# A ten-stage transformer kernel: another split of mixer 2's output product, 512-column down products, rounded masks and another placing of the modulation

## The chip, the cores and the metric

One core of one Trainium2 chip. Time is device microseconds of one execution. The kernel before ran three times: 1709.82, 1713.06 and 1714.77 us, median 1713.06.

## The reference

Two blocks of two layers each work on x (256 tokens by 1024), all in float32:

```
for l in 0, 1:                       # first block
    x += 0.5 * gate * swiglu(norm_mod(x))        # "ffn"
    x += gate * mixer(norm_mod(x))               # "mix1": recurrence, stick-breaking and forgetting attention
    x += 0.5 * gate * swiglu(norm_mod(x))        # "ffn"
for l in 0, 1:                       # second block
    x += gt1 * (group_rmsnorm([pool, chunk attention, top-k attention, latent attention]) @ w_out)   # "mix2"
    x += gt2 * ((silu(h @ w1) * (h @ w3)) @ w2)  # "ffn"
return rmsnorm(x)
```

Shifts, scales and gates of every norm come from `silu(c) @ w_ada` and `silu(c_2) @ w_mod`: 120 panels of 1 MB ("modulation").

## The kernel before, in words

The ten stages run in the order of SUBS: ffn, mix1, ffn, ffn, mix1, ffn, mix2, ffn, mix2, ffn (numbers 0 to 9). The work of each engine is written out by hand in one order, and the engines meet by semaphores.

x stands turned (features on partitions) as eight chunks X[:, c, :] of 128x256. Every large product is made exact with rounded operands: a weight w becomes WH (rounded to fp32r, by ScalarE, `hi_half`, L1146) and WL = w - WH (by VectorE, `lo_half`, recorded at L1602), an activation likewise HH and HL, AH and AL or YH and YL. One 128x128 block of weights then takes three matmuls of 256 columns: WH by AH, WH by AL, WL by AH. Weights come in units of 1 MB (two halves of eight blocks each) through `ring`, four slots filled by the sync queue in the order of `loads`; WH and WL hold four halves. A slot is free once VectorE has taken the remainders of its unit, or has used a modulation panel.

An ffn has 33 units: 22 for the up products (`cols`), 11 for the down product (`out_proj`, L661): eight output chunks c, each a sum over 22 blocks k, in PSUM banks 4, 5, 0, 1, 2, 3. `residual` on VectorE (L1689) adds each finished chunk to X, once, with the gate. Then `gained` makes the rounded operand of the next stage. Six stages are ffns, so there are six down stages of 176 blocks.

The modulation panels are multiplied and summed by VectorE (`ada_half`, L1629), 1024 columns at a time, at fixed ticks of the stages: ADA_N says how many panels a stage has, `ada_halves` at which tick. Eight more come at the start.

A mixer has 14 units: ten projections, four of the output product. `out_round` (L611) makes the output product in two rounds. A round sums over some of the eight input chunks for all eight output chunks. VectorE adds a chunk's first sum to X in `partial` and its second in the last loop, each followed by `gained`. In mix2, round 0 takes chunks 6, 7, 0, 1, 4, 5 and round 1 chunks 2, 3. The attention tiles behind a chunk must be normalised, turned and rounded before it can be used: `tile_scale` (ScalarE), `diagonal` (VectorE), `turned_out` (TensorE), `tile_out` (ScalarE), `tile_rest` (VectorE). Six attention scores with their softmax go through banks 2 and 3 one after the other (`mla_score`, `sa_score`, `ca_score`, then `maxima2`, `exponents2`, `turn`, `by_keys`, `attend`, `attended2`). All that order stands in mixer2 of TensorE (L1080 to L1098), ScalarE (L1514 to L1534) and VectorE (L2074 to L2116).

Masks are added to the scores as a matmul of the identity by the mask in full fp32 (`fox_score`, `stick_sums`, `sa_score`). Such a matmul stands in the trace as two instructions.

Of the kernel before, what the change touches and what calls it, by code (L numbers as in the profile page):

```python
# [14 lines left out]
S = 256  # L15
# [3 lines left out]
BIG = 1.0e30  # L19
# [10 lines left out]
def columns(spec):  # L30
    at, out = 0, {}
    for name, n in spec:
# [5 lines left out]
CONST_SPEC = [("ident", 128), ("ones", 128), ("eps", 1), ("one", 1), ("bd", 128), ("ntri", 128), ("partner", 96), ("rev", 128), ("cos", 256), ("sin", 256),  # L38
              ("cnt", 512), ("causal", 128), ("nones", 128), ("chunk", 256), ("sbpos", 128), ("sb01", 128),
              ("onehot", 320)]  # L40
CONST, NCONST = columns(CONST_SPEC)
FIRST = CONST["bd"]
# [15 lines left out]
ADA_N = (21, 3, 20, 20, 3, 20, 3, 20, 2, 0)  # L58
# [10 lines left out]
ROUNDS = {"mix1": ((0, 1, 2, 3), (6, 7, 4, 5)), "mix2": ((6, 7, 0, 1, 4, 5), (2, 3))}  # L69
# [5 lines left out]
def ada_halves(n, t):  # L75

    first = FIRST_ADA + sum(ADA_N[:n])
    halves = range(2 * ADA_N[n])
    if SUBS[n][0] == "ffn":
        at = [q for q in halves if 3 + q * (NTICK["ffn"] - 3) // len(halves) == t]  # L80
    else:
        at = [q for q in halves if ADA_AT[SUBS[n][0]][q // 2] == t]
    return [(first + q // 2, q % 2) for q in at]


def build(nc, A):
    ctx = ExitStack()
    with ctx:
# [15 lines left out]
        SQ = sb("SQ", [128, KD, S])  # L104
        CN = sb("CN", [128, NCONST])
        VC = sb("VC", [128, NVEC])
# [8 lines left out]
        AH = nc.alloc_sbuf_tensor_at("AH", [128, NF, S], F32R, offset=scr_at)  # L115
        AL = nc.alloc_sbuf_tensor_at("AL", [128, NF, S], F32R, offset=scr_at + 4 * NF * S)
# [25 lines left out]
        s_lam, s_lame, s_wfa = sem("s_lam"), sem("s_lame"), sem("s_wfa")  # L142
# [32 lines left out]
        eps = const("eps")  # L175
        one = const("one")
# [99 lines left out]
        SC = [scr(128), scr(256)]  # L276
        WK = [scr(128), scr(256)]
        CQ = v3(scr(512), 2)
# [65 lines left out]
        def summed2(n, r, c):  # L344
# [5 lines left out]
            if SUBS[n][0] == "mix1":  # L350
                return s_op2, 8 * SUBS[n][1] + 4 * r + c // 2 + 1
            return s_op2, 16 + 12 * SUBS[n][1] + 6 * r + c + 1 - (c > 3)
# [25 lines left out]
        def _(e):  # L378
            e.dma_start(VC[:, :], A["vecs"]).then_inc(s_vec, 16)
            e.dma_start(CN[:, 0:FIRST], A["consts"][:, 0:FIRST]).then_inc(s_const, 16)  # L380
# [7 lines left out]
            for p, (kind, i) in enumerate(loads):  # L388
# [16 lines left out]
                if p == 14:  # L405
                    e.dma_start(CN[:, FIRST:], A["consts"][:, FIRST:]).then_inc(s_const_rest, 16)
# [98 lines left out]
        def _(e):  # L505
# [139 lines left out]
            def turned_back(c):  # L645

                e.wait_ge(*((s_xg, c + 1) if c < KD - 1 else (s_xgl, 1)))
                for t in range(2):
                    last = e.transpose(PS[:, (6 if c < 4 else 0) + t, 128 * (c % 4):128 * (c % 4) + 128], XG[:, c, 128 * t:128 * t + 128], ident)
# [11 lines left out]
            def out_proj(n, xh, xl, ready):  # L661
# [4 lines left out]
                for i in range(KD * kt):  # L666
# [32 lines left out]
            def ffn(n):  # L699
# [10 lines left out]
                out_proj(n, lambda k: AH[:, k, :], lambda k: AL[:, k, :], lambda k: e.wait_ge(s_al, NF * j + k + 1))  # L710

            def mixer1(n):
# [32 lines left out]
                def fox_score(t):  # L745
# [3 lines left out]
                    for h in range(0, 4, per):  # L749
                        mm(s3[:, h:h + per, 128 * t:128 * t + 128], ident,  # L750
                           causal.rearrange("p (o k) -> p o k", o=1).to_broadcast([128, per, 128]), start=True, stop=False, skip=True)
# [5 lines left out]
                def fox_turn(t):  # L757

                    e.wait_ge(s_aex, a0 + t + 1)
                    for kt in range(t + 1):  # L760
# [6 lines left out]
                        for h in range(4):  # L767
                            last = e.transpose(PS[:, 6 + r % 2, 128 * h:128 * h + 128], softmax_of(t)[:, h, 128 * kt:128 * kt + 128], ident)
# [21 lines left out]
                def stick_sums(p):  # L790
                    e.wait_ge(s_zs, 2 * l + p + 1)
                    for h in (2 * p, 2 * p + 1):
# [3 lines left out]
                        last = mm(v3(c, 3)[:, 0:3:2, :], ident,  # L796
                                  const("sbpos").rearrange("p (o k) -> p o k", o=1).to_broadcast([128, 2, 128]),
# [68 lines left out]
            def mixer2(n):  # L866
# [32 lines left out]
                def index_rows():  # L899

                    for t in range(2):
                        last = e.transpose(PS[:, 7, 128 * t:128 * t + 128], SKI[:, 128 * t:128 * t + 128], ident)
# [1429 lines left out]
```

## Time and profile before

| | |
|---|---|
| median of three runs | 1713.06 us |
| profiled execution, its own time | 1709.39 us |
| its span | 1707.6 us |
| TensorE matmul busy | 1635.3 us, 96% |
| VectorE busy | 1313.3 us, 77% |
| ScalarE busy | 913.9 us, 54% |
| mean granted clock of TensorE | 0.984 |
| DMA | 403.22 MB, mean 236 GB/s |

The stages stand in the span in this order. The starts are those of the first product of each, read from the timeline: ffn 0 at 38, mix1 at 226, ffn 2 at 345, ffn 3 at 534, mix1 at 723, ffn 5 at 842, mix2 at 1032, ffn 7 at 1174, mix2 at 1365, ffn 9 at 1506 us. The down products are the last 62 us of each ffn. Busy time of TensorE counts overlapping matmuls once, so the number of instructions in a stretch tells more than the share.

### The profile page before, as it was taken

How to read it: one execution, taken by the hardware profiler on the slowest of the kernel's cores; microseconds unless marked ns; L12 is line 12 of the kernel's file. 1: busy time of each engine (PE TensorE's matmuls, PEld its weight loads, DVE VectorE, ACT ScalarE, POOL GpSimd, SP SyncE). 2: the span in 40 equal slices, each digit the busy share in tenths (PEclk: the TensorE clock that was granted, in tenths of full speed). 3: DMA queues.
4: the chain of work that ended last, by engine and by line, in shares of the span. 5: the costliest groups of instructions: out<-in, count | busy, mean ns of one | idle time of the engine just before them, and what ended most of it. 6: DMA issues, size and time to landing. Idle time of an engine off the chain costs nothing.

```text
span 1707.6 us, 31946 instructions
## 1 busy us (share of the span) xinstructions
PE 1635.3 (96%) x13290; PEld 1604.8 (94%) x13290; DVE 1313.3 (77%) x2071; ACT 913.9 (54%) x1564; POOL 84.0 (5%) x124
## 2 busy tenths in 40 slices
PE   2999999999999999999999999979999999899998
PEld 2999998999999999998999999978999998899998
DVE  6688898788788878897788888847888898385553
ACT  5445458664445544477554545646545456464453
POOL 4000000000000000000110001001000010010000
PEclk8999999999999999999999999989999999999999
DMA  9787765348786778754378888313778773145451
GB/s 357 301 317 300 300 253 198 124 178 336 294 317 261 300 300 316 290 210 173 115 271 312 305 318 301 124 50 117 301 300 319 296 250 124 50 149 197 176 196 50
DMA packets 57168, 403.22 MB, mean 236 GB/s; under 512 B 6606, under 2 KB 6866, under 8 KB 9280
## 3 DMA queue, kind: packets, MB, share of 16 engines
q1 hardware_dynamic: 55424, 396.01, 61.6%
q0 software_dynamic: 1600, 5.18, 1.0%
q8 instruction: 105, 1.72, 0.4%
q14 instruction: 39, 0.32, 0.1%
HBM read 400.10 MB, written 1.05 MB: 235 GB/s over the span
## 4 chain that ended last, share of the span: by engine, by line
PE 81%; DVE 11%; ACT 4%; issue 2%; DMA 1%; SPq 0%; DVEq 0%; ACTq 0%
PE PS L507 81%; DVE WL L1602 3%; DVE SCR L1602 2%; DVE SCR L1605 1%; ACT WH L1146 1%; DVE ring L1629 1%; ACT SCR L1429 1%; DMA SCR<-in_x 1%; DVE X L1605 1%; DVE HL L1605 1%; DVE SCR L1599 1%; DVE SMALL L1984 1%; DMA ring<-in_win 0%; ACT HH L1178 0%; DVE SCR L1946 0%
## 5 line engine op out<-in xcount | busy, mean ns | idle before, releaser
L1602 DVE TENSOR_TENSOR WL<-ring,WH 128x1024 fp32r<-128x1024 f32 (+1 forms) x508 | 599.8, 1215 | 187.4 <-ACT WH L1146 186.8
L507 PE MATMUL PS<-HH,WH 128*128 128x256 f32 (+1 forms) x2640 | 651.5, 285 | 12.7 <-ACT WH L1146 9.5
L507 PE MATMUL PS<-HL,WH 128*128 128x256 f32 (+1 forms) x2640 | 640.1, 283 | 0.0
L1146 ACT ACTIVATE WH<-ring 128x1024 fp32r<-128x1024 f32 (+1 forms) x508 | 510.9, 1048 | 100.1 <-PE PS L507 39.7
L507 PEld LDWEIGHTS PS<-HH,WH 128*128 128x128 f32 x2640 | 497.2, 190 | 18.8 <-ACT WH L1146 9.7
L507 PEld LDWEIGHTS PS<-HL,WH 128*128 128x128 f32 x2640 | 495.1, 190 | 0.7
L507 PE MATMUL PS<-HH,WL 128*128 128x256 f32 (+1 forms) x2640 | 375.9, 280 | 2.3 <-DVE WL L1602 2.2
L507 PEld LDWEIGHTS PS<-HH,WL 128*128 128x128 f32 x2640 | 339.4, 189 | 3.7 <-DVE WL L1602 3.7
L1629 DVE CUSTOM_DVE_ANT_0 ring<-ring,CB,VC 128x1024 f32<-128x1024 f32 x240 | 316.4, 1339 | 9.0 <-DMA ring<-in_ada 8.9
L507 PE MATMUL PS<-AH,WH 128*128 128x256 f32 x1056 | 297.5, 282 | 0.0
L507 PE MATMUL PS<-AL,WH 128*128 128x256 f32 x1056 | 297.0, 281 | 0.0
L507 PE MATMUL PS<-AH,WL 128*128 128x256 f32 x1056 | 297.0, 281 | 0.0
L507 PEld LDWEIGHTS PS<-AL,WH 128*128 128x128 f32 x1056 | 203.1, 192 | 0.0
L507 PEld LDWEIGHTS PS<-AH,WL 128*128 128x128 f32 x1056 | 199.0, 188 | 0.0
L507 PEld LDWEIGHTS PS<-AH,WH 128*128 128x128 f32 x1056 | 199.0, 188 | 0.0
L1204 ACT ACTIVATE AH<-SCR 128x256 fp32r<-128x256 f32 x132 | 55.2, 418 | 224.8 <-DVE SCR L1602 214.5
L1230 ACT ACTIVATE SCR<-PS 128x256 f32<-128x256 f32 x122 | 46.5, 381 | 114.5 <-PE PS L507 60.9
L437 POOL TENSOR_TENSOR SQ<-SQ 128x256 f32<-128x256 f32 x54 | 41.9, 776 | 1294.7 <-ACT SQ L1162 1292.5
L507 PE MATMUL PS<-SCR 128*128 128x64 f32 (+4 forms) x528 | 89.0, 315 | 5.9 <-DVE SQ L1602 4.4
L507 PEld LDWEIGHTS PS<-SCR 128*128 128x128 f32 (+1 forms) x528 | 77.1, 197 | 14.5 <-issue 8.7
L1605 DVE SCALAR_TENSOR_TENSOR X<-PS,MOD,X 128x256 f32<-128x256 f32 x112 | 53.0, 478 | 47.8 <-PE PS L507 47.5
L1159 ACT ACTIVATE HH<-X,AB 128x256 fp32r<-128x256 f32 x72 | 36.5, 506 | 93.2 <-DVE X L1605 92.7
(206 smaller groups left out, 1488.0 us busy)
## 6 DMA issues: line engine op xcount, KB each, us to landing
ring<-in_up SPq DMA_DIRECT2D x88, 1024.0 KB, 5.6
ring<-in_ada SPq DMA_DIRECT2D x72, 1024.0 KB, 7.2
ring<-in_ffn SPq DMA_DIRECT2D x66, 1024.0 KB, 4.8
ring<-in_mod SPq DMA_DIRECT2D x48, 1024.0 KB, 6.9
ring<-in_down SPq DMA_DIRECT2D x44, 1024.0 KB, 6.5
ring<-in_win SPq DMA_DIRECT2D x32, 1024.0 KB, 6.9
ring<-in_wout SPq DMA_DIRECT2D x16, 1024.0 KB, 4.8
ring<-in_winv SPq DMA_DIRECT2D x4, 1024.0 KB, 4.8
```

What stands on the lines that cost most here:

```text
L437: e.tensor_tensor(SQ[:, c, :], SQ[:, c - 1, :], SQ[:, c, :], ALU.add).then_inc(s_psum, 1)
L507: return e.matmul(out, lhsT, rhs, start=start, stop=stop, skip_group_check=skip)
L1146: e.activation(half_of(i)[0], slot_of(("unit", u))[:, w * (i % 2):w * (i % 2) + w], ACT.Copy).then_inc(s_hi, 1)
L1159: e.activation(HH[:, c, 0:S], X[:, c, :], ACT.Copy, scale=AB[:, 8 * m + c:8 * m + c + 1]).then_inc(s_yh, 1)
L1204: e.activation(AH[:, f, :], G6[:, 3 + f % 3, :], ACT.Copy).then_inc(s_ah, 1)
L1230: e.activation(G6[:, f % 3, :], PS[:, up_bank(f), 0:256], ACT.Silu).then_inc(s_silu, 1)
L1429: last = e.activation(p3[:, h, :], s3[:, h, :], ACT.Exp, bias=st[:, at + h:at + h + 1], scale=scale, accum_out=st[:, 8 + h:9 + h])
L1599: return e.tensor_scalar(out, a, s1, s2, op0) if s2 is None else e.tensor_scalar(out, a, s1, s2, op0, op1)
L1602: return e.tensor_tensor(out, a, b, op)
L1605: return e.scalar_tensor_tensor(out=out, in0=a, scalar=s, in1=b, op0=op0, op1=op1)
L1629: ins = e.tensor_tensor_reduce(out=w, in0=w, in1=CB[:, 0 if i < 72 else 1, :], scale=1.0, scalar=bias, op0=ALU.mult, op1=ALU.add, accum_ou ...
L1984: ins = e.tensor_reduce(st[:, 0:4], score_bank(n, 2, t), AX.X, ALU.max, negate=True)
```

## The change

- The down products of output chunks 0 to 6 take AH and AL side by side (new layout AHL) as one 512-column matmul by WH, then WL by AH on the first 256 columns. The two halves of the bank are added to X by two instructions instead of one. Chunk 7 is left as it was.
- mix2: round 0 takes chunks 6, 7, 0, 1 and round 1 chunks 4, 5, 2, 3. The last two scores, three `attend`, two `turn` and four `turned_out` are issued between the output chunks of round 0. On ScalarE and VectorE roundings of output weights (units u0+10 to u0+14) are moved around them, in part by halves.
- identity, causal mask, stick-breaking mask and the top-k mask are rounded to fp32r (BIG becomes a power of two), so that mask products are fp32r. Transposes read the same identity bits as fp32.
- ADA_N: from (21, 3, 20, 20, 3, 20, 3, 20, 2, 0) to (22, 2, 20, 21, 0, 22, 0, 21, 0, 4). The four of the last ffn lie in its up products.

```diff
-ADA_N = (21, 3, 20, 20, 3, 20, 3, 20, 2, 0)
+ADA_N = (22, 2, 20, 21, 0, 22, 0, 21, 0, 4)
-ROUNDS = {"mix1": ((0, 1, 2, 3), (6, 7, 4, 5)), "mix2": ((6, 7, 0, 1, 4, 5), (2, 3))}
+ROUNDS = {"mix1": ((0, 1, 2, 3), (6, 7, 4, 5)), "mix2": ((6, 7, 0, 1), (4, 5, 2, 3))}
 # out_proj, TensorE
-                    mm(out, wh[:, g, :], xh(k), start=k == 0, stop=False)
-                    mm(out, wh[:, g, :], xl(k), start=False, stop=False)
+                    if c < KD - 1:
+                        both = PS[:, banks[c % len(banks)], :]
+                        mm(both, wh[:, g, :], AHL[:, k, :, :].rearrange("p a s -> p (a s)"), start=k == 0, stop=k == kt - 1, skip=True)
+                    else:
+                        mm(out, wh[:, g, :], AH[:, k, :], start=k == 0, stop=False)
+                        mm(out, wh[:, g, :], AL[:, k, :], start=False, stop=False)
...
-                    last = mm(out, wl[:, g, :], xh(k), start=False, stop=k == kt - 1)
+                    last = mm(out, wl[:, g, :], AH[:, k, :], start=False, stop=k == kt - 1, skip=c < KD - 1)
 # residual, VectorE
-                stt(X[:, c, :], PS[:, banks[c % 6], 0:256], MOD[:, 24 * n + 16 + c:24 * n + 17 + c], X[:, c, :], ALU.mult,
+                b = (4, 5, 0, 1, 2, 3)[c % 6]
+                if c < KD - 1:
+                    step(stt(X[:, c, :], PS[:, b, 256:512], MOD[:, 24 * n + 16 + c:24 * n + 17 + c], X[:, c, :], ALU.mult, ALU.add))
+                stt(X[:, c, :], PS[:, b, 0:256], MOD[:, 24 * n + 16 + c:24 * n + 17 + c], X[:, c, :], ALU.mult,
                     ALU.add).then_inc(s_x, 1)
 # sa_score; fox_score and stick_sums likewise
-                        mm(s3[:, h:h + per, :], ident, WK[t][:, 0:m].rearrange("p (o k) -> p o k", o=1).to_broadcast([128, per, m]),
+                        mm(s3[:, h:h + per, :], identr[:, :], WKR[t][:, :].rearrange("p (o k) -> p o k", o=1).to_broadcast([128, per, m]),
 # mixer2, TensorE
-                turned_out(n, o0 + 4)
-                e.wait_ge(s_toe_ca, 64 * (l + 1))
-                e.wait_ge(s_proj, p0 + 10)
-                ca_score(a0 + 4, 0)
-                attend(a0 + 3, 1, r0 + 6, o0 + 5, of_sa)
-                turn(a0 + 4, 0, r0 + 6)
-                ca_score(a0 + 5, 1)
-                attend(a0 + 4, 0, r0 + 7, o0 + 6, of_ca)
-                turned_out(n, o0 + 5)
+                e.wait_ge(s_proj, p0 + 9)
                 out_round(n, 0, {
-                    1: (lambda: turned_out(n, o0 + 6),),
-                    2: (lambda: turn(a0 + 5, 1, r0 + 7),),
-                    4: (lambda: attend(a0 + 5, 1, r0 + 9, o0 + 7, of_ca),),
+                    0: (lambda: e.wait_ge(s_toe_ca, 64 * (l + 1)), lambda: e.wait_ge(s_proj, p0 + 10), lambda: ca_score(a0 + 4, 0)),
+                    1: (lambda: attend(a0 + 3, 1, r0 + 6, o0 + 5, of_sa), lambda: turn(a0 + 4, 0, r0 + 6), lambda: ca_score(a0 + 5, 1)),
+                    2: (lambda: attend(a0 + 4, 0, r0 + 7, o0 + 6, of_ca), lambda: turned_out(n, o0 + 4), lambda: turn(a0 + 5, 1, r0 + 7)),
+                    3: (lambda: attend(a0 + 5, 1, r0 + 9, o0 + 7, of_ca),),
+                    4: (lambda: turned_out(n, o0 + 5),),
+                    5: (lambda: turned_out(n, o0 + 6),),
                     6: (lambda: turned_out(n, o0 + 7),),
                 })
 # mixer2, ScalarE: hi(u0 + 11) no longer ahead of tile_out(o0 + 3)
-                hi(u0 + 11)
                 tile_out(n, o0 + 3)
                 by_keys(r0 + 4, 0, a0 + 3)
                 by_keys(r0 + 5, 1, a0 + 3)
-                tile_out(n, o0 + 4)
+                hi_half(2 * u0 + 22)
                 exponents2(a0 + 4, 0, 1.0, r0 + 4)
+                hi_half(2 * u0 + 23)
...
 # mixer2, VectorE
                 selected(1)
+                lo(u0 + 10)
                 pooled(1, o0 + 3)
-                lo(u0 + 10)
                 tile_rest(n, o0 + 1)
...
+                maxima2(a0 + 3, 1)
                 diagonal(n, o0 + 4)
-                maxima2(a0 + 3, 1)
+                gates(n)
                 tile_rest(n, o0 + 3)
-                lo(u0 + 11)
-                tile_rest(n, o0 + 4)
+                lo_half(2 * u0 + 22)
                 maxima2(a0 + 4, 0)
+                partial(n, 0)
+                lo_half(2 * u0 + 23)
```

Not shown: the order of the constants in their tensor, three short roundings of constants on ScalarE in ffn 0, and the placing of the last units' roundings, which for u0+14 becomes that of mix1.

## Rows read from the trace of the kernel before

**Rows 1.** The page: busy time, share and instructions of TensorE; the chain's engines.
```profile
PE 1635.3 (96%) x13290; PEld 1604.8 (94%) x13290; DVE 1313.3 (77%) x2071; ACT 913.9 (54%) x1564; POOL 84.0 (5%) x124
...
PE 81%; DVE 11%; ACT 4%; issue 2%; DMA 1%; SPq 0%; DVEq 0%; ACTq 0%
```
**Rows 2.** Windows: length, busy PE PEld DVE ACT POOL (count), clock, DMA.
```profile
163.80:226.00 62.20, 62.20 (x530) 62.20 (x530) 52.46 (x72) 29.89 (x40) 4.43 (x6) 1.00 0.78 308
...
1032.16:1174.50 142.34, 130.57 (x974) 123.48 (x973) 101.21 (x218) 77.54 (x191) 6.55 (x10) 0.95 0.43 148
1364.62:1505.94 141.32, 130.41 (x975) 123.56 (x973) 98.70 (x214) 77.64 (x191) 6.54 (x10) 0.95 0.40 142
...
722.67:842.40 119.73, 113.71 (x872) 108.14 (x870) 94.91 (x156) 81.09 (x149) 4.47 (x5) 0.99 0.45 163
1126.70:1174.50 47.80, 40.89 (x314) 39.28 (x313) 23.48 (x48) 24.58 (x67) 1.48 (x2) 0.93 0.25 86
...
1131.00:1137.00 6.00, 5.22 (x25) 5.25 (x25) 3.97 (x7) 1.59 (x4) 0.00 (x0) 0.50 0.34 108
```
**Rows 3.** Waits of TensorE in mix2, 1104 to 1174.5: total us, times, longest.
```profile
PE PS L507 <- DVE YL L1605: 6.8, 3, 3.4
...
PE PS L507 <- DVE X L1605: 1.8, 2, 1.3
```
**Rows 4.** The chain of waits in mix2: start, us, what.
```profile
1112.40 0.33 DVE SQ L1602
1112.73 1.69 DVE WL L1602 x2
...
1129.31 1.04 ACT WH L1146
...
1131.78 7.02 PE PS L507 x36
```
**Rows 5.** Timeline of TensorE: start, time, matmul, tiles, shape, count.
```profile
1148.12 0.28 PE L507 MATMUL PS<-YH,WH 128*128 128x256 f32 x1
...
1148.69 0.28 PE L507 MATMUL PS<-YH,WL 128*128 128x256 f32 x1
...
1430.44 1.02 PE L507 MATMUL PS<-SCR,CN 128*128 128x512 f32 x2
1431.31 0.38 PE L507 MATMUL PS<-SCR 128*128 128x128 f32 x2
...
259.82 0.28 PE L507 MATMUL PS<-HH,WFH 128*4 128x256 f32 x1
...
260.75 0.28 PE L507 MATMUL PS<-HH,WFH 128*4 128x256 f32 x1
```
**Rows 6.** The page's groups: loads of 128 weight columns, mean ns.
```profile
L507 PEld LDWEIGHTS PS<-AH,WL 128*128 128x128 f32 x1056 | 199.0, 188 | 0.0
```
**Rows 7.** The tile WFH: loads of 4 weight columns, ns min/median/max.
```profile
L507 PEld LDWEIGHTS PS<-HH,WFH x16: 83/84/85, 259.7 to 757.9; 128*4 128x4 f32 x16
```
**Rows 8.** Groups of VectorE in the first down stage, 163.8 to 226.
```profile
L1602 DVE TENSOR_TENSOR WL<-ring,WH 128x1024 fp32r<-128x1024 f32 x22 | 26.0, 1216 | 2.0 <-ACT WH L1146 1.9
L1629 DVE CUSTOM_DVE_ANT_0 ring<-ring,CB,VC 128x1024 f32<-128x1024 f32 x15 | 21.8, 1474 | 0.0
...
L1605 DVE SCALAR_TENSOR_TENSOR X<-PS,MOD,X 128x256 f32<-128x256 f32 x7 | 3.3, 478 | 2.6 <-PE PS L507 2.6
```
**Rows 9.** Waits of all engines in the same stretch.
```profile
ACT WH L1146 <- DMA ring<-in_down: 12.6, 7, 4.5
DVE HL L1605 <- ACT HH L1159: 3.5, 6, 0.6
```
**Rows 10.** The chain of waits in the second mix1.
```profile
760.97 1.20 DVE ring L1629
...
762.17 1.20 DVE ring L1629
```
**Rows 11.** Timeline of ScalarE in the second mix1.
```profile
763.71 1.72 ACT L1336 ACTIVATE SCR<-SCR,SMALL 128x256 f32<-128x256 f32 x4
```

More of the change, by code:

```diff
@@ L79, in ada_halves @@
     if SUBS[n][0] == "ffn":
-        at = [q for q in halves if 3 + q * (NTICK["ffn"] - 3) // len(halves) == t]
+        ticks = NF - 3 if n == NSUB - 1 else NTICK["ffn"] - 3
+        at = [q for q in halves if 3 + q * ticks // len(halves) == t]
     else:
@@ L104, in build @@
         SQ = sb("SQ", [128, KD, S])
+        cn_at = nc.sbuf_base
         CN = sb("CN", [128, NCONST])
+        identr, causalr, sbposr = (nc.alloc_sbuf_tensor_at(k + "r", [128, 128], F32R, offset=cn_at + 4 * CONST[k])
+                                   for k in ("ident", "causal", "sbpos"))
         VC = sb("VC", [128, NVEC])
@@ L276, in build @@
         SC = [scr(128), scr(256)]
+        wk_at = scr_at + 4 * Scratch.at
         WK = [scr(128), scr(256)]
+        WKR = [nc.alloc_sbuf_tensor_at(f"WKR{t}", [128, 128 * (t + 1)], F32R, offset=wk_at + 512 * t) for t in range(2)]
         CQ = v3(scr(512), 2)
@@ L648, in turned_back @@
                 for t in range(2):
-                    last = e.transpose(PS[:, (6 if c < 4 else 0) + t, 128 * (c % 4):128 * (c % 4) + 128], XG[:, c, 128 * t:128 * t + 128], ident)
+                    last = e.transpose(PS[:, (6 if c < 4 else 0) + t, 128 * (c % 4):128 * (c % 4) + 128], XG[:, c, 128 * t:128 * t + 128], ident1)
                 if c % 4 == 3:
@@ L659, in token_sums, with out_proj @@
                     last.then_inc(s_fss, 1)
[L661 removed]
+            def out_proj(n, ready):
                 kt = depth_of(n)
@@ L749, in fox_score @@
                     for h in range(0, 4, per):
-                        mm(s3[:, h:h + per, 128 * t:128 * t + 128], ident,
-                           causal.rearrange("p (o k) -> p o k", o=1).to_broadcast([128, per, 128]), start=True, stop=False, skip=True)
+                        mm(s3[:, h:h + per, 128 * t:128 * t + 128], identr[:, :],
+                           causalr[:, :].rearrange("p (o k) -> p o k", o=1).to_broadcast([128, per, 128]), start=True, stop=False, skip=True)
                     for h in range(4):
@@ L1226, in ffn @@
                         e.activation(CB[:, 1, :], CB[:, 1, :], ACT.Silu).then_inc(s_cb, 1)
+                        e.wait_ge(s_const_rest, 16)
+                        for exact, k in ((identr, "ident"), (causalr, "causal"), (sbposr, "sbpos")):
+                            e.activation(exact[:, :], const(k), ACT.Copy).then_inc(s_exact, 1)
                     if f >= 3:
@@ L2090, in mixer2 @@
                 attended2(a0 + 4, o0 + 6)
-                tile_rest(n, o0 + 5)
+                partial(n, 2)
+                tile_rest(n, o0 + 4)
                 diagonal(n, o0 + 6)
-                gates(n)
-                partial(n, 0)
-                lo(u0 + 12)
-                partial(n, 1)
-                tile_rest(n, o0 + 6)
-                partial(n, 2)
                 partial(n, 3)
                 attended2(a0 + 5, o0 + 7)
+                lo_half(2 * u0 + 24)
                 partial(n, 4)
+                tile_rest(n, o0 + 5)
                 diagonal(n, o0 + 7)
                 partial(n, 5)
-                lo(u0 + 13)
+                tile_rest(n, o0 + 6)
+                lo_half(2 * u0 + 25)
                 partial(n, 6)
```

59 lines of the change are left out of this document (32 added, 27 removed).

## The prediction

> **What bounds the kernel now.** I read the page first: TensorE is busy for 96% of the span and the chain that ended last lies for 81% on it [rows 1]. So time goes only where TensorE does less, or where it waits. Second, the windows by stage [rows 2]. In a down stage the clock is 1.00 and TensorE has no pause: 530 matmuls in 62.20 us, 117.4 ns from start to start. An ffn can gain only by fewer or shorter products. The mixers are different: mix2 takes 142.34 and 141.32 us at a mean clock of 0.95, and VectorE is busy for 101.21 of the 142. Third, the waits of TensorE and the chain inside mix2 [rows 3, 4] say where those pauses are.
>
> The sum goes by the profiled execution: 1709.39 us, 1.8 us more than its span. The median of the runs is 1713.06, 3.7 above it, and I put the saving under the median.
>
> **Wide down products.** Chunks 0 to 6 of 22 blocks in six stages are 7 x 22 x 6 = 924 blocks. Before, a block costs three matmuls, 3 x 117.4 = 352 ns [rows 2]. After, it costs one of 512 columns and one of 256. No fp32r matmul of 512 columns stands in the trace, so I bound it. 256 columns at 2.4 GHz are 107 ns, so 10 ns of the 117 are something else. The mask products of 512 columns in fp32 start 1431.31 - 1430.44 = 0.87 us apart for two instructions, 0.435 us each [rows 5], at two clocks per column (427 ns): there only some 8 ns come on top of a stream twice as long as that of a 512-column fp32r product. Is the weight load the limit? A load of 128 columns takes 188 ns and one of 4 columns 84 [rows 6, 7], 104 ns less, but the products with the 4-column weights still follow each other at (260.75 - 259.82) / 8 = 116 ns [rows 5]. So the load is hidden and a longer stream hides it as well. In the output rounds the pitch is (1148.69 - 1148.12) / 5 = 114 ns [rows 5]. If the extra 10 ns belongs to the columns, the wide product costs 235 and nothing is gained. If nothing came on top of the stream, the block would cost 320 and save 32 ns. The nearest rows say half an fp32 instruction, 218 ns, and 115 for the narrow one: 333, a saving of 19 ns. 924 x 19 = 17.6 us. Ends: 0 and 29.6 us.
>
> The Trainium skill, "TensorE: Matmul & The Clock Gate", section "Back-to-back issue gap", gives N/2.4 + 2.5 ns once warm, so 109 and 216 ns. The trace does not agree at 256 columns (117.4). By that rule a block would cost 325 ns, the saving would be 25 us and the total some 7 us lower than mine; it is a rival below.
>
> What hides the second addition to X? VectorE. It is busy for 52.46 of the 62.20 us [rows 2]. Seven more additions of 478 ns [rows 8], less where they overlap, with seven waits for the first one to finish, are 3.2 us. The moved modulation adds up to one panel of two instructions per down stage, 2 x 1.47 = 2.9 us at the mean [rows 8]. VectorE then has 56 to 59 us of work and still waits 3.5 us in all for ScalarE's HH [rows 9], while TensorE would need only 62.2 - 154 x 0.019 = 59.3 us. That is too tight for nothing to show. What is queued behind the new wait on VectorE is the next `lo_half`, `gained` and the modulation, and by the modulation the slots of the ring. ScalarE already waits 12.6 us for panels in the first down stage [rows 9]. The four halves of WH and WL cover delays of a few us. I charge 0.6 us for each of the five down stages that have modulation, 3 us in all (ends 0 and 10). Net of the wide products: 14.6 us.
>
> **Masks in fp32r.** One fp32 mask product of 512 columns costs 0.87 us [rows 5], in fp32r 0.22 (from the 218 above); one of 256 costs half, 0.43, against 0.115. In mix1 the causal masks are 1 x 512 and 2 x 256, the stick-breaking ones 4 x 256: 0.65 + 6 x 0.32 = 2.5 us per mixer, 5.0 for both. There TensorE runs without pause, but one later wait is for VectorE, so I keep 4 us (ends 2 and 5). In mix2 there are three of 512 columns: 2 us per mixer, counted below. Transposes cost what they did.
>
> **Modulation out of the mixers.** In the second mix1 two modulation instructions of 1.20 us stand in the chain of waits [rows 10], inside a stretch in which only VectorE moves. Without them the chain is 2.4 us shorter, until ScalarE's exponentials (763.71 + 1.72 = 765.43 [rows 11]) end last; VectorE used them at 767.62, so the gain is 2.2 us. The first mix1 keeps its two panels on that place and gains nothing. In mix2 the three panels stand early, where TensorE is mostly busy: 0.3 us each. The panels themselves cost nothing in up products, where VectorE has room, and the four in the last ffn end before its gates are needed. Sum 2.8 us.
>
> **mix2's tail.** The window from 1126.70 to the end is 47.80 us with 314 matmuls [rows 2]. Of these 192 belong to the output rounds, 192 x 0.1155 = 22.2 us. The other 122 are fp32 instructions of the late attention, 114 at about 0.11 and 8 of 256 columns at 0.216: 14.3 us. Work is 36.5 us, so 11.3 us are waits and half clock. Two of the three waits for YL, 5.1 of the 6.8 us, and 1.8 us for X [rows 3] lie there, and the clock is 0.50 from 1131 to 1137 [rows 2], which costs 3 us. Small restarts, 1.4 us, make up the rest.
>
> What follows in the new order, step by step:
> - Before, `turned_out(o0+4)` waited until 1131.78, since `tile_rest(o0+3)` stood behind two ScalarE roundings of unit u0+11, the second at 1129.31 [rows 4]. They now come after `tile_out(o0+3)`, so YL is ready 2.1 us earlier, and TensorE has chunks 6 and 7 of the first output to do meanwhile. About 0.8 of 3.5 us is left.
> - `ca_score(a0+4)` then runs. While VectorE and ScalarE make its softmax (0.7 + 1.5 us), TensorE does output chunk 1 and `attend(a0+3)`, 3.2 us of work: hidden.
> - `ca_score(a0+5)` takes 3.5 us; its softmax (1.2 + 1.9 us) lies beside chunk 2 (1.4), `attend(a0+4)` (0.9) and `turned_out(o0+4)` (0.4): 0.5 us late for `turn(a0+5)`.
> - ScalarE must then do `tile_scale`, `tile_out` and two `by_keys`, 2.8 us, beside `turn` and chunk 3 (2.3): 0.5 us late. Every later `turned_out` has a chunk of 1.4 us ahead of it.
> - Round 1 has four products per chunk, 1.4 us, against the 0.9 us that VectorE needs for X and HL. Before it had 0.7 us, which is where the waits for X came from. The next ffn starts 0.5 us quicker.
> - TensorE no longer stands for 3 us, so I expect the second half-clock stretch to go.
>
> New tail: 36.5 + 0.8 + 0.5 + 0.5 + 1.2 of restarts = 39.5 us, 8.3 less, and 0.5 in the next ffn. Ahead of the tail, the masks save 2 us, but `lo(u0+10)` now stands before `pooled(1)`. In the chain it was 1112.40 for `pooled`, then the rounding [rows 4]. The new order delays `pooled(1)` by 2.3 us, and behind it ScalarE's `tile_scale(o0+3)` and `tile_out(o0+1)`, so `turned_out(o0+2)` comes 1.7 us later. Net 0.3. Per mix2 9.1 us, for both 18.2 (ends 9 and 25).
>
> **Sum.** 14.6 + 4 + 2.8 + 18.2 = 39.6 us. 1709.4 - 39.6 = 1669.8 beside the profile, 1713.1 - 39.6 = 1673.5 as a median.
>
> **Rivals.**
> - The extra 10 ns belongs to the columns. For it: it is in every fp32r stream, with full and with 4-column weights. Against it: fp32 streams have only 8 ns on 427. The wide products then give nothing, and the additional work on VectorE 1 us: 1713.1 - 25.0 + 1.0 = 1689. Chance 0.14.
> - Nearly nothing comes on top of a stream once the weight load has time: 325 ns a block, 25 us, which VectorE then limits to about 20: 1668, and with the full mixer gain 1662. Chance 0.20. This is also what the skill's rule would give.
> - The late attention only moves its waits: in round 0 `turn(a0+5)` and `attend(a0+5)` wait for a ScalarE that is now behind with halves of weights, and the half clock stays. Mix2 then gives 3 us each: 1713.1 - 39.6 + 12.2 = 1686. For it: softmax takes 3.1 us per step and only 2.7 lie beside it. Chance 0.12.
> - Slower: VectorE becomes the bound of the down stages. Its 56 to 59 us plus 3.5 of waits reach 62.5, more than the 62.2 of now; TensorE then waits in pieces, and if such a wait brings a stretch at 1.2 GHz like that from 1131 to 1137 [rows 2], 3 us more are lost. The mixers and masks give 25 us, so it decides from 4.2 us lost in each of six stages. At 5 us each (2 of waits and 3 of clock): 1713.1 - 25 + 30 = 1718. Against it: the clock is 1.00 in the whole stage, and four halves lie ready. Chance 0.03.
>
> My own forecast has 0.51. A difference of over 0.3%, 5 us, can be told from no change. Faster by more than that: 0.95; within it 0.02; slower 0.03. The range takes in the first three rivals and half of the bounds: 1654 to 1692.
>
> **What would show it.** In the changed profile: 512-column matmuls from AHL with starts about 218 ns ahead of the next; down stages of 59 to 60 us with the clock at 1.00; VectorE busy for over 90% of them; mix2 of about 132 us, with waits for YL of under 2 us and no half clock in its last 40 us; mask products of 0.22 us; no modulation in the second mix1 which takes 115 to 116 us instead of 119.7. I am wrong if the wide product starts 235 ns ahead of the next, if TensorE waits over 2 us for WL in the down stages, or if mix2 stays above 137 us.

## The result and the profile after

The changed kernel takes 1691.84 us (median of 4 runs, 1688.75 to 1694.38), the kernel before in the same comparison 1713.91 (1709.82 to 1714.86). The ratio is 0.9876, 95% interval 0.9864 to 0.9887: 22 us faster, where 39.6 was forecast. The profiled execution took 1691.13 us, against 1709.39 of the one before: 18.3 us less. What follows explains these 18.3; the medians are 3.8 further apart. The profiled execution of the kernel before, 1709.39 us, was faster than all four of its timed runs.

The page of the changed kernel answers to [rows 1]: 944 fewer matmuls and weight loads (924 by the wide products, 20 by the masks), and only 13.7 us less busy time of TensorE. The second line is the group of products from the new layout AHL: 924 of 512 columns and 264 of 256.

```profile
PE 1621.6 (96%) x12346; PEld 1552.1 (92%) x12346; DVE 1333.8 (79%) x2113; ACT 912.1 (54%) x1567; POOL 85.0 (5%) x124
...
L516 PE MATMUL PS<-AHL,WH 128*128 128x512 f32 (+1 forms) x1188 | 373.5, 371 | 0.0
```

Windows of the changed kernel, with the columns of [rows 2]: the first down stage, that of ffn 5, the second mix1, the first mix2, its tail, the second mix2.

```profile
163.81:228.63 64.82, 62.99 (x377) 55.09 (x375) 55.70 (x78) 28.68 (x40) 4.43 (x6) 1.00 0.81 306
967.87:1032.08 64.21, 62.59 (x377) 54.93 (x375) 55.46 (x78) 28.89 (x40) 4.44 (x6) 1.00 0.80 311
723.91:838.98 115.07, 110.44 (x865) 105.18 (x863) 90.02 (x147) 81.92 (x150) 4.21 (x5) 1.00 0.41 150
1032.08:1164.93 132.85, 125.77 (x972) 121.16 (x970) 96.79 (x208) 78.75 (x193) 8.69 (x12) 0.97 0.37 130
...
1125.67:1164.93 39.26, 37.99 (x315) 36.72 (x313) 24.53 (x47) 24.98 (x68) 3.63 (x4) 1.00 0.23 81
...
1354.76:1487.92 133.16, 126.06 (x972) 121.42 (x971) 96.15 (x208) 79.08 (x193) 8.90 (x12) 0.96 0.37 129
```

The down stage has lost 153 matmuls and got 2.6 us longer than the 62.20 of [rows 2]. The first mix2 is 9.5 us shorter. Its tail, from `turned_out(o0+3)` on in both kernels (1126.7 before, 1125.67 now), is 39.26 us at full clock instead of 47.80 at 0.93.

With every stage taken from the start of its first product to that of the next one's, and without the 18.1 us before TensorE's first instruction (18.2 now), the account is this:

| us | before | after | measured | forecast |
|---|---|---|---|---|
| six down stages (the last with the final norm) | 384.6 | 389.4 | +4.8 | -14.6 |
| four mixers (with masks and modulation) | 521.9 | 497.7 | -24.2 | -25.0 |
| six up stages | 782.9 | 784.0 | +1.1 | 0 |
| span | 1707.6 | 1689.3 | -18.3 | -39.6 |

No product of the up stages is changed. Their lengths differ by 1.5 us between profiles, also where they are the same code (that of ffn 3 takes 126.2 or 127.7 us), because 256-column products follow each other for long stretches sometimes at 113, sometimes at 118 ns.

Timeline of TensorE in the first down stage of the changed kernel (start, time, matmul, tiles, shape, count):

```profile
169.80 0.40 PE L516 MATMUL PS<-AHL,WH 128*128 128x512 f32 x1
170.04 0.28 PE L516 MATMUL PS<-AHL,WL 128*128 128x256 f32 x1
170.16 0.40 PE L516 MATMUL PS<-AHL,WH 128*128 128x512 f32 x1
170.39 0.28 PE L516 MATMUL PS<-AHL,WL 128*128 128x256 f32 x1
```

Only the starts are to be read. Over the stretches looked at (325 blocks) the wide product starts 235 ns ahead of the next, the narrow one 118. A block costs 353 ns, as before. That is rival 1.

The narrow products have a second pace, which the wide ones don't reach. In chunk 7 of the last down stage of the changed kernel, with full clock, three of them take 1675.17 - 1674.83 = 0.34 us, 113 ns each:

```profile
1674.83 0.39 PE L516 MATMUL PS<-AHL,WH 128*128 128x256 f32 x2
1675.06 0.28 PE L516 MATMUL PS<-AHL,WL 128*128 128x256 f32 x1
1675.17 0.39 PE L516 MATMUL PS<-AHL,WH 128*128 128x256 f32 x2
```

In the kernel before 80 of the 176 blocks of that stage take 340 ns, in e10, with three products of the same size from AHL, none. The blocks with a wide product stay at 353 in all stages but for single ones. So beside the faster pace the wide form costs 13 ns a block. What chooses the pace is not shown.

Waits of the first down stage (engine, tile, line, waited for: us in total, times, longest):

```profile
ACT WH L1155 <- DMA ring<-in_down: 15.1, 6, 5.1
...
DVE WL L1617 <- ACT WH L1155: 2.9, 2, 1.5
PEld PS L516 <- DVE WL L1617: 2.7, 3, 1.6
PE PS L516 <- DVE WL L1617: 1.8, 2, 1.3
```

The chain of the end of the same stage (start, us, what) shows how that comes about:

```profile
206.90 1.69 DVE ring L1644
...
208.63 4.92 DMA ring<-in_down
...
213.58 1.07 ACT WH L1155
...
214.67 2.36 DVE WL L1617 x2
217.03 0.41 DVE X L1620
...
217.47 0.49 DVE X L1620
```

A slot of the ring comes free only when VectorE has used the panel in it (206.90). The next unit lands 4.92 us later, ScalarE rounds it, VectorE takes the remainder, and only then come the two additions to X. Each further instruction on VectorE delays the slot, and the DMA turns that into a later WL. TensorE then stands before a product that needs WL. In the whole kernel it waited for WL 4 times before, 2.2 us in all, and now 10 times, 6.9 us.

Waits of TensorE in the first mix2 from 1104 us on; they answer to [rows 3]:

```profile
PE PS L516 <- DVE SQ L1617: 4.7, 1, 4.7
PE PS L516 <- DVE YL L1620: 0.9, 2, 0.6
PE PS L1008 <- ACT SCR L1441: 0.6, 1, 0.6
```

The 6.8 us for YL and 1.8 for X have gone down to 0.9. The wait for SQ, 2.2 us before, has become 4.7: `attend(a0+2)` waits for `pooled(1)`, as e4 and e10 bear out.

### The profile page after: what moved, and what is told of

Its sections match the earlier page's. It is cut to its first block, busy times and chain, and to the rows that moved or that the text cites. A ratio compares the mean times of both kernels' runs of the same rounds, so it can differ in the third digit from the quotient of the medians.

```text
span 1689.3 us, 30111 instructions
## 1 busy us (share of the span) xinstructions
PE 1621.6 (96%) x12346; PEld 1552.1 (92%) x12346; DVE 1333.8 (79%) x2113; ACT 912.1 (54%) x1567; POOL 85.0 (5%) x124
## 4 chain that ended last, share of the span: by engine, by line
PE 77%; DVE 13%; ACT 5%; DMA 3%; issue 1%; SPq 0%; DVEq 0%; ACTq 0%
PE PS L516 76%; DVE WL L1617 4%; DVE ring L1644 2%; ACT WH L1155 2%; DMA ring<-in_down 1%; DVE X L1620 1%; DVE SCR L1617 1%; DVE SCR L1620 1%; DVE HL L1620 1%; DMA SCR<-in_x 1%; ACT SCR L1441 1%; DVE SCR L1614 1%; DVE SMALL L2001 1%; DMA ring<-in_win 0%; ACT HH L1168 0%
## 5 line engine op out<-in xcount | busy, mean ns | idle before, releaser
L516 PE MATMUL PS<-AHL,WH 128*128 128x512 f32 (+1 forms) x1188 | 373.5, 371 | 0.0
L516 PE MATMUL PS<-AHL,WL 128*128 128x256 f32 x1056 | 297.4, 282 | 4.0 <-DVE WL L1617 3.9
L516 PEld LDWEIGHTS PS<-AHL,WH 128*128 128x128 f32 x1188 | 213.8, 188 | 42.2
L516 PEld LDWEIGHTS PS<-AHL,WL 128*128 128x128 f32 x1056 | 198.3, 188 | 6.4 <-DVE WL L1617 6.1
L1213 ACT ACTIVATE AHL<-SCR 128x256 fp32r<-128x256 f32 x132 | 55.1, 418 | 225.3 <-DVE SCR L1617 215.1
L1620 DVE SCALAR_TENSOR_TENSOR X<-PS,MOD,X 128x256 f32<-128x256 f32 x154 | 73.3, 479 | 25.4 <-PE PS L516 22.9
L516 PE MATMUL PS<-YH,WH 128*128 128x256 f32 x256 | 73.8, 288 | 1.1 <-DVE YL L1620 1.1
L516 PE MATMUL PS<-YL,WH 128*128 128x256 f32 x256 | 71.5, 279 | 0.0
```

Source lines behind the costliest of these rows:

```text
L516: return e.matmul(out, lhsT, rhs, start=start, stop=stop, skip_group_check=skip)
L1213: e.activation(AH[:, f, :], G6[:, 3 + f % 3, :], ACT.Copy).then_inc(s_ah, 1)
L1620: return e.scalar_tensor_tensor(out=out, in0=a, scalar=s, in1=b, op0=op0, op1=op1)
```

## The experiments

All compare with the kernel before, run beside them on the same chip. "Changed" is the changed kernel, and each diff is against it, except where it says before. This table gives the stage lengths from each profile, in us; the text refers to it.

| kernel | ratio, 95% | down 0 | down 5 | mix1 | mix1 | mix2 | mix2 |
|---|---|---|---|---|---|---|---|
| before | 1 | 62.2 | 62.2 | 118.5 | 119.7 | 142.3 | 141.3 |
| changed | 0.9876 (0.9864-0.9887) | 64.8 | 64.2 | 116.6 | 115.1 | 132.9 | 133.2 |
| e1 narrow | 0.9843 (0.9829-0.9858) | 62.3 | 62.4 | 116.6 | 115.8 | 132.1 | 133.7 |
| e2 old modulation | 0.9865 (0.9847-0.9883) | 62.7 | 62.2 | 116.6 | 118.3 | 132.5 | 133.6 |
| e3 one addition | 0.9838 (0.9823-0.9853) | 62.2 | 62.2 | 116.6 | 115.8 | 132.5 | 132.3 |
| e4 pooled first | 0.9857 (0.9835-0.988) | 64.6 | 64.2 | 118.3 | 115.9 | 130.6 | 130.8 |
| e5 wide alone | 1.0004 (0.9991-1.0017) | 62.6 | 62.2 | 118.6 | 118.6 | 142.4 | 141.5 |
| e6 mix2 alone | 0.9907 (0.9893-0.992) | 62.2 | 62.2 | 119.6 | 118.6 | 134.6 | 134.0 |
| e7 masks alone | 0.9964 (0.9949-0.998) | 62.2 | 62.2 | 116.6 | 116.7 | 140.6 | 138.8 |
| e9 narrow, pooled first | 0.9826 (0.9813-0.984) | 62.2 | 62.2 | 117.8 | 115.8 | 131.3 | 130.3 |
| e10 early pooled | 0.9813 (0.98-0.9827) | 62.2 | 62.2 | 118.2 | 115.8 | 129.1 | 127.9 |
| e11 no modulation in mix1 | 0.9822 (0.9808-0.9835) | 62.2 | 62.2 | 120.0 | 114.7 | 128.5 | 128.0 |

### Which factor lengthens the down stages: e1, e2, e3

e1, the down products narrow and one addition per chunk:
```diff
-                    if c < KD - 1:          # out_proj: wide product
+                    if c < 0:
...
-                if c < KD - 1:              # residual: two additions
+                if c < 0:
```


> The changed kernel with three 256-column down products and one addition per chunk again; all else as changed. The theory (fp32r costs by the column, the second addition makes VectorE late): down stages 0 and 5 fall from 64.8 and 64.2 us to below 63, no product waits for WL in them, and the total is 4 to 6 us below the changed kernel, ratio to before 0.984 to 0.985. Rival (the 22 panels of modulation alone make VectorE late): those stages stay above 64 us and the total stays at 0.987 to 0.988. Rival (the wide product does save time): total above 1692 us.

Measured: 1688.38 us, ratio 0.9843. Its timeline in the first down stage, with the layout AHL and two narrow products where the wide one was:

```profile
170.02 0.28 PE L516 MATMUL PS<-AHL,WL 128*128 128x256 f32 x1
170.13 0.40 PE L516 MATMUL PS<-AHL,WH 128*128 128x256 f32 x2
170.37 0.28 PE L516 MATMUL PS<-AHL,WL 128*128 128x256 f32 x1
170.49 0.40 PE L516 MATMUL PS<-AHL,WH 128*128 128x256 f32 x2
```

Two products of 256 columns take the 235 ns of the wide one. TensorE doesn't wait for WL in that stage any more, though it has 22 panels: panels alone don't make VectorE late. The wide form gains nothing, and taking it out with its second additions gives back 3.5 us by the medians and 5.7 by the ratios.

e2, the modulation as before:
```diff
-ADA_N = (22, 2, 20, 21, 0, 22, 0, 21, 0, 4)
+ADA_N = (21, 3, 20, 20, 3, 20, 3, 20, 2, 0)
```


> The changed kernel with the modulation panels at their old places (21, 3, 20, 20, 3, 20, 3, 20, 2, 0). The theory (22 panels and two additions together are too much): down stages 0 and 5 at 62.3 to 62.8 us, but the second mix1 2 us longer again, mix2 up to 1 us: total within 2 us of the changed kernel. Rival (the second addition alone does it): the down stages 0 and 5 stay above 64 us and the total is 2 to 3 us above the changed kernel.

Measured: 1691.13 us, as the changed kernel. The down stages 0 and 5 fall to 62.7 and 62.2, and the second mix1 rises to 118.3 (in part by two stretches of 3.4 us at half clock, which the changed kernel's profile doesn't have): the one pays for the other.

e3, the wide products kept, but only the first half of each bank is added to X, so that the part from AL is left out of the result for these chunks:
```diff
-                if c < KD - 1:              # residual: two additions
+                if c < 0:
```


> The changed kernel, but only the first 256 columns of a wide sum are added to X: the part WH by AL is left out of X. The theory (VectorE's second addition is the cost): down stages as in e1, 62.2 to 62.6 us, total as e1 within 1.5 us. Rival (a 512-column product holds TensorE or a bank longer than two of 256): down stages 0 and 5 above 64 us.

Measured: 1686.98 us, 0.9838. The window of its first down stage:

```profile
163.80:226.00 62.20, 62.20 (x377) 55.07 (x376) 53.13 (x73) 29.45 (x40) 4.43 (x6) 1.00 0.82 319
```

377 matmuls without a pause in the same 62.20 us as the 530 of [rows 2]. That is the cleanest reading of the case: with no wait at all the wide products save nothing. The rival, that a wide product holds TensorE or a bank longer, is out for this pace. The lengthening needs both the second additions and 22 panels in the stage; without either it is at most 0.5 us.

### Each part alone: e5, e6, e7

e5 is the kernel before with the wide products and their two additions only; e6 is before with the new rounds and orders of mix2 only; e7 is before with the rounded masks only.

> The kernel before with the 512-column down products and their second addition alone; modulation, masks and mix2 as before. The theory (fp32r costs by the column, 235 and 118 ns a block as before; the additions only fill VectorE): down stages 62.2 to 63 us, total 0 to 3 us above the kernel before. Rival (my prediction's step, 19 ns a block saved, hidden in the changed kernel by late weights): down stages near 60 us and the total 10 us or more lower.

> The kernel before with the two rounds of four chunks and the late attention steps of mix2 alone. By the prediction: each mix2 7 us shorter (8.8 without the 2 us of masks), total 14 to 16 us less, ratio 0.991. Rival (the order helps only with the masks and without modulation in the mixer): each mix2 less than 5 us shorter.

> The kernel before with the fp32r masks alone. By the prediction: each mix1 2.0 to 2.5 us and each mix2 about 2 us shorter, 8 us in all, ratio 0.995. Rival (VectorE and ScalarE pace the mixers there): less than 4 us in all.

Measured: 1713.34, 1696.19 and 1707.05 us. The wide products are worth 0 (interval -0.9 to +1.7 thousandths, that is -1.5 to +2.9 us). The new order of mix2 shortens the two stages by 7.7 and 7.3 us, the masks the four mixers by 1.9, 3.0, 1.7 and 2.5 us. These four add up to 9.1 us, the ratio says 6.2 (3.4 to 8.7): the profiled execution of e7 was its fastest. Not all of the 3.0 belongs to the masks, since the kernel before has a stretch of 3.4 us at half clock in its second mix1, and e7 has none. Without any, and without the new masks, that stage takes 118.6 us in e5 and in e6, and the first mix1 of e5 too:

```profile
227.33:345.95 118.62, 112.68 (x873) 107.07 (x872) 97.07 (x158) 82.02 (x150) 4.28 (x5) 1.00 0.47 170
```
```profile
721.33:838.05 116.72, 110.34 (x865) 105.48 (x863) 95.57 (x157) 80.96 (x149) 4.22 (x5) 1.00 0.46 167
```

The first line is the first mix1 of e5, the second the second mix1 of e7, both at clock 1.00. At equal clock the masks are worth 1.9 to 2.0 us in each mix1. In mix2, e7's second stretch at half clock is 3.4 us long instead of 6.8, which is part of its 1.7 and 2.5.

The three ratios multiply to 0.9875, and the changed kernel has 0.9876. That leaves nothing for the new placing of the modulation, but the intervals together allow 4 to 5 us either way. The direct comparison is e2, where the down stages take what the second mix1 gets.

### The wait before attend(a0+2): e4, e9, e10

e4 (and e9, with narrow products besides):
```diff
                 selected(1)
-                lo(u0 + 10)
                 pooled(1, o0 + 3)
+                lo(u0 + 10)
```


> The changed kernel with VectorE's rounding of unit u0+10 behind the first pooled(1) again, as before the change. The theory (in the changed trace TensorE stands for 4.9 us before attend(a0+2), which waits for that pooled(1)): this wait falls to 2.5 us, the next one grows from 0.6 to about 1.3, and each mix2 is 1.5 us shorter: total 3 us less, ratio 0.985 to 0.986. Rival (VectorE has the same work either way and TensorE waits for the later tile_rest): total unchanged within 1 us.

Measured: 1691.3 us. Its waits in the same part of the first mix2:

```profile
PE PS L516 <- DVE SQ L1617: 2.5, 1, 2.5
PE PS L516 <- DVE YL L1620: 1.8, 3, 1.0
```

The wait for `pooled(1)` is 2.5 us again, and 0.9 us of the gain comes back as waits for YL. The mix2 stages are 2.3 and 2.4 us shorter, more than the 1.3 that the two waits give. In the second, the half-clock stretch is 6.8 us long instead of 10.2. The median doesn't show it (1685.9 to 1694.2 is a wide scatter, and this profile has two stretches of 3.4 us at half clock in the first mix1 where the changed kernel's has none), and the ratios 0.9857 and 0.9876 have intervals that overlap; the stages and e9 do show it.

> The changed kernel with narrow down products and, in the second mixer, pooled(1) before lo(u0+10) instead of behind it. Theory (the two costs are separate: the wide products' waits in down stages 0 and 5, and the remainder of FeedForward chunk 10 that delays pooled(1)): down stages 0 and 5 at 62.2 to 62.4 us, second mixers 130.6 to 131 us each, that is 3.5 us for the first and 2 x 2.3 for the second: ratio to the kernel before 0.981 to 0.983. Rival (the remainder moved behind pooled(1) comes late for the FeedForward product that reads it, or the down stages are shortened already by the order): no better than the narrow kernel alone, 0.9843.

Measured: 1685.03 us, 0.9826, down stages at 62.2, mix2 at 131.3 and 130.3, each 0.3 outside the bounds. The two gains add: against e1 3.4 us by the medians and 4.2 by the two stages.

e10, narrow products, and in mix2:
```diff
-                largest(1, (6, 7))
-                selected(1)
-                lo(u0 + 10)
+                largest(1, (6,))
                 pooled(1, o0 + 3)
+                largest(1, (7,))
                 tile_rest(n, o0 + 1)
                 diagonal(n, o0 + 3)
+                selected(1)
                 attended2(a0 + 2, o0 + 4)
+                lo(u0 + 10)
```


> As the run with narrow products and pooled(1) first, but the VectorE work ahead of pooled(1) in the second mixer is cut further: only largest(1,(6,)) stands before it, and largest(1,(7,)), tile_rest(o0+1), selected(1) and lo(u0+10) come in between and after. Theory (attend(a0+2) waits for pooled(1) on VectorE and for nothing else): the wait of 2.6 us before it shrinks to about 0.8, second mixers 128.8 to 129.3 us, ratio 0.979 to 0.981. Rival (VectorE's work in the block is fixed, so that the wait moves to the next product that needs selected(1) or to tile_rest): the wait comes back at the first reader of the moved steps with 1.5 to 2 us, second mixers 130.5 to 131, ratio as with pooled(1) first.

Measured: 1681.67 us (1679.55 to 1682.6, 4 runs), ratio 0.9813, the fastest of all: 32 us below the kernel before and 10 below the changed one. Its waits in the first mix2, the whole stage:

```profile
PE PS L516 <- DVE YL L1620: 2.0, 3, 1.3
PE PS L516 <- DVE SQ L1617: 0.8, 1, 0.8
...
PE PS L516 <- DVE WKR L1614: 0.2, 1, 0.2
```

The wait for SQ is down from 4.7 to 0.8 us and doesn't come back at the mask that `selected(1)` makes (WKR, 0.2 us); waits for YL take 1.1 us more than in the changed kernel. The theory held for the wait, and the stages took 129.1 and 127.9 us, against 128.8 to 129.3. The ratio fell just outside its bounds, with an interval (0.98 to 0.9827) that reaches into them. The first mix1 took 118.2 us, with a stretch at half clock that the changed kernel's profile doesn't have; but that doesn't explain the ratio, since this profile is the fastest of the four runs.

### Two panels fewer in the first mix1: e11

```diff
-ADA_N = (22, 2, 20, 21, 0, 22, 0, 21, 0, 4)     # and as e10
+ADA_N = (24, 0, 20, 21, 0, 22, 0, 21, 0, 4)
```


> As the run with early pooled(1), with the two modulation panels that are left in the first first-mixer (ADA_N 22, 2) moved to the down stage before it (24, 0). Theory (two panels in a mixer cost TensorE their products, as the second first-mixer showed: 4.6 us shorter than before where masks alone gave 3.0): first first-mixer 114.3 to 115 us instead of 116.6, down stage 0 the same as with 22 panels: 1.5 to 2.2 us, ratio 0.978 to 0.980. Rival (24 panels are too much work for VectorE and the DMA ring in one down stage, as 22 were with the wide products): down stage 0 gets 2 us or more longer, and nothing is gained.

Measured: 1682.53 us, 0.9822: a miss for the theory, and for the rival as to the place. The down stage stays at 62.2, but the next stage takes 120.0 us, 1.8 more than in e10. One thing went as foreseen: the wait of 2.0 us for ScalarE that the first mix1 has in e10, and the second one had in the kernel before the modulation left it, is gone. More was lost at the start of the stage. The chain there:

```profile
225.19 1.68 DVE ring L1644
...
226.91 5.71 DMA ring<-in_win
...
232.65 1.06 ACT WH L1155
233.71 0.40 ACT HH L1168
234.10 0.32 ACT SQ L1171
```

VectorE's last panels free the slots late, the projection weights land late, ScalarE waits for them in order, and behind it stand the HH and the square that TensorE needs. TensorE waits 2.5 us, and then the granted clock is at the lower of its two levels, 1.2 GHz, for 3.4 us. This window holds most of that stretch, and so has a mean of 0.57:

```profile
234.40:237.80 3.40, 3.34 (x15) 3.23 (x16) 3.13 (x5) 2.44 (x5) 0.00 (x0) 0.57 0.16 43
```

### Whose are the extra ten nanoseconds: e8, e12

e8 reads the 512-column operand and its weights as bfloat16, the upper halves of the same words; e12 does so with the 256-column product by WL as well.
```diff
-                        mm(both, wh[:, g, :], AHL[:, k, :, :].rearrange("p a s -> p (a s)"), ...)
+                        mm(both, wh[:, g, :].bitcast(b16)[:, 1:256:2], AHL[:, k, :, :].rearrange("p a s -> p (a s)").bitcast(b16)[:, 1:1024:2], ...)
```


> The changed kernel, but the 512-column products read only the upper 16 bits of weights and activations as bf16 (at the same addresses, a step of two elements); this makes the down products coarse. If a 4-byte element read at each column is what costs 235 instead of 213 ns, and the type decides it, they start about 216 ns ahead of the next. If the distance between columns in memory decides it, they stay at 235 ns or more.

Measured (one run): 1701.74 us. The products alternate in type, and the timeline of TensorE in its first down stage reads:

```profile
170.30 0.40 PE L516 MATMUL PS<-AHL,WH 128*128 128x512 bf16 x1
170.34 0.48 PE L516 MATMUL PS<-AHL,WL 128*128 128x256 f32 x1
170.66 0.40 PE L516 MATMUL PS<-AHL,WH 128*128 128x512 bf16 x1
```

A block takes 360 ns, longer than 353. It couldn't be told from that whether the type, the step of two elements or the change between types costs the time, so e12 took the change away.

> As the run that read the 512-column operand as bfloat16, but the 256-column product of the same block is read as bfloat16 too (the upper halves of the same words, with a step of two elements), for output chunks 0 to 6 of the down products. The output loses the lower parts of these products. In the stretch the type no longer changes from product to product. Theory (the 10 ns over 107 for 256 columns belong to the columns of an fp32r stream): with both in bfloat16 a block costs 216 to 218 + 109 to 115 ns = 325 to 333 ns, and the down stage without modulation, the last one, 69 to 70 us instead of 73; in the others VectorE and the ring may hold TensorE back. Rival 1 (the columns cost 0.459 ns in any type, the rate is the array's): 353 ns a block. Rival 2 (reading with a step of two elements costs time): over 360 ns a block, as in the run with mixed types.

Measured (one run): 1688.68 us. Its timeline in the first down stage, and a weight load there in the down stage of ffn 3 (ns min/median/max):

```profile
170.13 0.39 PE L516 MATMUL PS<-AHL,WH 128*128 128x512 bf16 x1
170.35 0.28 PE L516 MATMUL PS<-AHL,WL 128*128 128x256 bf16 x1
170.47 0.39 PE L516 MATMUL PS<-AHL,WH 128*128 128x512 bf16 x1
```
```profile
L516 PEld LDWEIGHTS PS<-AHL,WH x197: 96/97/192, 662.1 to 722.7; 128*128 128x128 bf16 x153, 128*128 128x128 f32 x44
```

Over 307 blocks the median is 225 ns for 512 columns, 114 for 256, and 340 ns a block. That is 13 less than with a wide product in fp32r at the same addresses, and neither the theory (325 to 333) nor a rival had it. Rival 1 (353 ns in any type) and rival 2 (over 360 ns) are out with their numbers. In bfloat16 too 256 more columns cost 225 - 114 = 111 ns, not 107, and only some 3 ns are left for the instruction. The down stage of ffn 3 took 60.9 us, the last one 72.5 (69 to 70 expected).

Three things stay open. The type changed together with the step and with the weight load (97 ns instead of 188), so it is not shown which of them gives the 13 ns. No run reads bfloat16 without a step, so a price of the step below that of rival 2 can't be excluded. And 340 ns a block is no privilege of bfloat16: three narrow fp32r products reach it too, as chunk 7 above shows; only with the wide one in fp32r it doesn't come.

## Why the prediction was wrong

The measured 1691.84 us lie at the very end of the range, 1654 to 1692. **The step that failed** is the price of the wide product. I put it at "half an fp32 instruction, 218 ns", because that was the nearest row, and 115 for the narrow one. Measured are 235 and 118. The term was 17.6 us saved, ends 0 and 29.6; the lower end came true. Ruling out the load by the 4-column weights [rows 5] stands, but it left two causes, a time per instruction and a time per column, and the row of 256 columns can't tell them apart. The fp32 instruction [rows 5], which I took to decide it, was the wrong neighbour: it takes 427 ns for 512 columns anyhow, and a limit of 0.459 ns a column (235 for 512) would never show in it. What the kernel before did hold is a sign that the 10 ns is no constant: the pitch is 117.4 in the down stages and 114 in the output rounds [rows 2, 5], with products of the same type and size. A stretch at the lower level of the clock, 1.2 GHz, doesn't decide it either. Here one of the kernel before, in its first mix1 (granted clock 0.50), as a timeline of TensorE:

```profile
280.07 0.41 PE L507 MATMUL PS<-HH,WH 128*128 128x256 f32 x1
...
280.71 0.39 PE L507 MATMUL PS<-HL,WH 128*128 128x256 f32 x1
```

The second line is three products further on. There 256 columns follow each other at (280.71 - 280.07) / 3 = 0.213 us, and 256/1.2 is 213 ns: nothing comes on top. A slowest pace of 0.459 ns a column, well under the 0.833 of that clock, would be hidden there; but so would a time per instruction that is only seen at the upper level. No wide product fell into such a stretch. What e1 and e3 show is that the excess grows with the columns, about 11 ns over 107 for 256 and 22 over 213 for 512; why is open.

The rule of the Trainium skill ("TensorE: Matmul & The Clock Gate", section "Back-to-back issue gap", N/2.4 + 2.5 ns at 2.4 GHz, there called the gap of a single product by itself) gives 216 ns for 512 columns. This case's trace does not agree, with 235; in bfloat16 it is 225, nearer but not there.

**The charge on VectorE** was 3 us over the five stages with modulation. They got 5.5 us longer (the sixth is 0.8 shorter), and that beside a TensorE that is no faster; beside the quicker one that I expected it would have been more. The mechanism was the one foreseen: the modulation and with it the slots of the ring. The distribution was not. It falls on the two stages that have 22 panels (+2.6 and +2.0), while those with 20 and 21 lose 0.2 to 0.4. VectorE was busy for 55.7 us (56 to 59 foreseen), 86% of the stage: a mean share below 90% was enough for waits, since the delay comes through the ring.

**Rival 1** said 1689 and had 0.14; measured 1691.8. The charge on VectorE, 1 us in it and 5.5 in five stages in fact, is more than that difference.

**Masks.** Forecast 4 us for both mix1. Measured are 4.9 (e7, 1.9 + 3.0), of which 3.9 at equal clock, as said at e7. For both mix2, 4 us forecast and 4.2 measured (1.7 + 2.5), again with some clock in it. The prices held too. The first causal mask of the first mix1, before and after, each with the instruction behind it:

```profile
286.12 1.13 PE L507 MATMUL PS<-CN 128*128 128x512 f32 x2 [0.78 <-DVE SCR L1605]
287.09 1.05 PE L507 MATMUL PS<-SCR 100*128 100x128 f32 x8
```
```profile
288.69 0.50 PE L516 MATMUL PS<-causalr,identr 128*128 128x512 f32 x1 [1.11 <-DVE SCR L1620]
289.03 1.05 PE L516 MATMUL PS<-SCR 100*128 100x128 f32 x8
```

At this place the pair of fp32 instructions takes 0.97 us and the fp32r one 0.34, so 0.63 us are saved, where 0.65 was the forecast. The start-to-start times are both longer than the prices in the sum (0.87 and 0.22): both products stand behind a wait and a change of type.

**Modulation.** 2.2 us forecast for the second mix1. Between e7 (masks alone, 116.7) and the changed kernel (115.1), both without a stretch at half clock in it, lie 1.6. In e11, also without one, the stage takes 114.7, which makes it 2.0. The other profiles with the new placing have one of 3.4 us and take 115.8 to 115.9. The up products took the panels for nothing, as said; the down stages did not.

**mix2.** Forecast 9.1 us each, measured 9.5 and 8.2 (e6 and e7 add to 9.4 and 9.8); about 132 us forecast, measured 132.9. The second gained less, and its half-clock stretch ahead of the tail is 10.2 us long instead of 6.8. The tail was to be 39.5 us and is 39.3. The wait for the YL of `tile_rest(o0+3)`, which now stands inside the first output chunk, is 0.6 us by the waits (forecast 0.8), that before `turn(a0+5)` 0.6 (0.5), `attend(a0+5)` doesn't wait (0.5), and the half-clock stretch in it is gone, the tail's clock being 1.00. Ahead of the tail, moving `lo(u0+10)` before `pooled(1)` was foreseen to delay it by 2.3 us; the wait grew by 2.5 and e4 gave 2.3 and 2.4 back. Rival 3, that the late attention only moves its waits, is out: it gave 3 us each, and e6 alone gives 7.7 and 7.3.

**Slower.** VectorE did come to bound two down stages, but by 2 to 2.6 us, and at full clock: no stretch at 1.2 GHz followed.

Open is what makes the wide fp32r product cost 22 ns more than its columns at 2.4 GHz, and why the narrow ones run at 113 instead of 118 ns in long stretches.

## What to carry to other kernels

Before counting on fewer, wider instructions, find out whether the overhead seen in the pitch belongs to the instruction or to the column: compare the pitch of the same type at different widths, look whether it differs from stretch to stretch, and don't borrow the rest from another type. If the type has no product of the width in question, a kernel that differs in nothing else is the only witness. Where a transfer waits for a slot that a busy vector engine frees, additional work on it costs at the far end of the ring, one or two steps later and perhaps in the next stage, at a busy share of 86%. And in a hand-written order, look for what stands before the one instruction that another engine waits for: taking three steps from before `pooled(1)` shortened mixers of 132.1 and 133.7 us (e1) by 3.0 and 5.8 (e10); part of the second is a half-clock stretch of 3.4 us instead of 10.2.

## What the runs showed of the hardware

- In the down stages, at granted clock 1.00, a 512-column fp32r product starts 235 ns ahead of the next one and two of 256 columns take the same (2 x 117.6); 377 matmuls take the same 62.20 us as 530 (e3). In other stretches, such as the end of the changed kernel's last down stage, 256-column products start 113 ns apart; blocks with a 512-column one stay at 353 ns.
- At granted clock 0.50 the 256-column products start 213 ns apart, which is 256/1.2.
- The same addresses read as bfloat16 with a step of two take 225 and 114 ns (e12, one run); alternating bfloat16 and fp32r costs 360 ns a block (e8, one run) against 340 (all bfloat16) and 353 (all fp32r, with a wide product).
- A load of 128 weight columns takes 97 ns as bfloat16 and 188 as fp32r. Beside loads of 84 ns the fp32r pitch of 256 columns is still 116 [rows 5, 7].
- An fp32r mask product of 512 columns saves 0.63 us against the two fp32 instructions at the same place.
